# Second attention layer of a two-layer block: queries split where they are made, scores issued one item ahead, the gate product moved to the front, the sums of shares moved to GpSimd

## The chip, the cores and the metric

One Trainium2 chip, one core of it. The metric is device time of one launch in microseconds (us). Engines are named as in the profile: PE is TensorE (PEld its weight loads), DVE is VectorE, ACT is ScalarE, POOL is GpSimd, SP is SyncE, which here issues all the DMAs.

## The reference

A sequence of 1024 rows of 1024 features passes two blocks. The change is in the last attention of the second one, a banded attention with 16 heads of 64, two key/value heads and a sink per head, followed by a gate:

```
def swa_sink_mixer(h, kb, vb, pos_bias, mask, w_in, sinks, w_out):
    q, z = jnp.split(h @ w_in, 2, axis=-1)
    q = q * (HEAD_DIM ** -0.5)
...
    def block_fn(args):
        qn, kn, vn, mn = args
        s = jnp.einsum('bqhgd,bkhd->bhgqk', qn, kn).astype(jnp.float32) + pos_bias
        s = jnp.where(mn[None, None, None], s, NEG_INF)
        m = jnp.maximum(jnp.max(s, axis=-1, keepdims=True), sink)
        p = jnp.exp(s - m)
        p = p / (jnp.sum(p, axis=-1, keepdims=True) + jnp.exp(sink - m))
        return jnp.einsum('bhgqk,bkhd->bqhgd', p.astype(vn.dtype), vn)
...
    return (o * jax.nn.silu(z)) @ w_out
```

Each block of 128 queries sees the 128 keys before it and its own 128, so a row of scores is 256 wide.

## The kernel before

Every product is made in three matmuls: each fp32 operand is held as a high part (`...h`, a copy rounded to fp32r) and a low part (`...l`, the operand minus its high part), and high*high, high*low and low*high are summed in PSUM. ACT makes the high parts, DVE or POOL the low ones.

Every engine has a program written out by hand, stage after stage (`pe_keys`, `act_keys`, ... and then `pe_window`, `act_window`, `dve_window`, `pool_window`, `sp_window`, and then `..._final`). Engines run in order and wait on semaphores by named events: `self.at("q2hi", j)` is the event "high part of query tile j is ready", set where the instruction that makes it says `up(("q2hi", j))`. The SP engine issues DMAs in order and waits in order too.

The projection stage (`..._keys`) makes, after keys and values, 16 units `("b", j)` of 128 features by 1024 rows: units 0 to 7 are queries, units 8 to 15 the gate. ACT copies each from PSUM into one of five tiles `tmp` (queries scaled by 0.125, gate through Silu) and SP stores it in a DRAM scratch `qd`. The weights of each unit are loaded to `raw`, and split into `wh` (ACT) and `wl` (POOL), some units ahead.

The window stage (`..._window`) is a software pipeline over 32 items n = (j, m): query tile j holds two heads, m is a pair of query blocks. `pipeline(32, [(lag, f), ...])` runs step s = 0, 1, ... and in each step calls every f(s - lag) in the order in which the list has them; so in one step an engine works on several items, and the order of the list is the order in its queue. The work on one item, with its lag:

- PE `score` (lag 0): 12 matmuls k2h/k2l by q2h/q2l into two PSUM halves, one for each head.
- DVE `top` (0): four custom instructions (line 103) that add the bias table `t`, negate, write to `tmp` and reduce the row's minimum to `st`.
- POOL `sink` (0): a 128x4 addition. ACT `exps` (0): four Exp with row sums, and one of 128x4 for the sinks.
- DVE `norm` (2): the 128x4 sum of the row sums and the sinks' exponentials, and its reciprocal. POOL `norm` (2): the 128x1024 product of the exponentials with the reciprocal.
- PE `turn` (3): eight transposes into PSUM. ACT `turned` (3): two copies to p2h. DVE `turned_low` (3): two subtractions to p2l.
- PE `values` (4): up to 20 matmuls with the values; two items share one PSUM half.
- Every second item, lag 5: DVE `stored` multiplies the output by the gate tile `zs`, ACT `stored` makes o2h, POOL `stored_low` o2l, SP `zload` reloads `zs` for the next pair, once o2l is made.
- Every fourth item, lag -2 (`begin`): the next query tile, loaded by SP into `tmp[4]`, is split by ACT (q2h) and DVE (q2l). The two pairs of query tiles `qb` alternate. The second pair lies where an operand of the projection was, so it can't be written before unit ("b", 15) is done (`QZ`).

The final stage is the output projection (`("bo", ...)`, matmuls o2h/o2l by wh/wl) and the last normalization.

Of the kernel before, what the change touches and what calls it, by code (L numbers as in the profile page):

```python
# [7 lines left out]
F32 = mybir.dt.float32  # L8
FR = mybir.dt.float32r
ALU = mybir.AluOpType  # L10
# [134 lines left out]
class Net:  # L145
# [36 lines left out]
    def setup(self):  # L182
# [3 lines left out]
        for i in range(6):  # L186
            self.add_slot(3 + i)
        self.tmp = [self.sb(f"tmp{i}", 10 + i) for i in range(5)]
        if "ps" not in self.mem:
            self.mem["ps"] = [self.nc.alloc_psum_tensor(f"ps{i}", [128, S], F32) for i in range(4)]  # L190
        self.halves = [Half(t[:, h * 512:h * 512 + 512]) for t in self.mem["ps"] for h in (0, 1)]
# [94 lines left out]
        self.gates = self.dram("gates", [2048, S])  # L286
        self.xs = self.dram("xs", [S, S])
        self.hd = self.dram("hd", [22 * 128, S])
        self.qd = self.dram("qd", [2048, S])
# [2400 lines left out]
    def sp_keys(self, e):  # L2690
        self.half_units(e, "pl", 256, self.sp_w)
        self.sp_w(e, "k2")
        self.sp_w(e, "v2")
        e.wait_ge(*self.at("kx", 1))
        e.dma_start(self.kx0[64:128, :], self.kx0[0:64, :]).then_inc(self.sig["kx0"].up(("kxt", 0)), 16)
        e.dma_start(self.kx1[0:64, :], self.kx1[64:128, :]).then_inc(self.sig["kx1"].up(("kxt", 1)), 16)
        self.sp_w(e, ("b", 0))
        self.sp_w(e, ("b", 1))
        for j in range(NT):
            for h in (0, 1):  # L2700
                e.wait_ge(*self.at("sum", "n4", h, j))
            e.dma_start(self.xs[j * 128:j * 128 + 128, :], self.X[j][:, :]).then_inc(
                self.sig[f"xs{j}"].up(("xs", j)), 16)
        for j in range(16):
            if j == 3:
                e.wait_ge(*self.at("gst"))
                e.wait_ge(*self.at(*self.POOL_OUT))
                for kv in range(2):
                    self.sp_table(e, f"t2{kv}", self.T2[kv], 8 + 8 * kv)
            if j == 14:  # L2710
                e.wait_ge(*self.at("t3free", 9))
                e.wait_ge(*self.at("qd", 0))
                e.dma_start(self.tmp[4][:, :], self.qd[0:128, :]).then_inc(self.sig["ld4"].up(("ql2", 0)), 16)
            if j >= 2:
                self.sp_w(e, ("b", j))
            i = self.b_tmp(j)
            e.wait_ge(*self.at("bcopy", j))
            e.dma_start(self.qd[j * 128:j * 128 + 128, :], self.tmp[i % 5][:, :]).then_inc(
                self.sig[f"st{i % 5}"].up(("qd", j), ("t3free", i)), 16)

    def b_tmp(self, j):
        return j if j < 14 else j + 1

    def act_keys(self, e):
        for event in self.POOL_TMP:
# [25 lines left out]
        for j in range(16):  # L2751
            if j in (6, 8):
                self.act_flip(e, "t2%d" % (j // 2 - 3), self.T2[j // 2 - 3])
            if j == 10:
                for i in range(NT):
                    e.wait_ge(*self.at("xs", i))
                for kv in (0, 1):
                    self.act_keys2(e, kv)
            if j == 12:
                e.wait_ge(*self.at("zv2"))  # L2760
                e.wait_ge(*self.at("prod", "v2t"))
                for kv in (0, 1):
# [4 lines left out]
            i = self.b_tmp(j)  # L2767
            e.wait_ge(*self.at("prod", ("b", j)))
            if i < 5:
                e.wait_ge(*self.at("nlo", "n4", 3, 1, 6))  # L2770
                e.wait_ge(*self.at("nlo", "n4", 3, 1, 7))
            elif i == 19:
                pass
            else:
                e.wait_ge(*self.at("t3free", i - 5))
            done = self.sig["evac"].up(("bcopy", j), ("free", ("b", j)))
            if j < 8:
                e.activation(self.tmp[i % 5][:, :], self.ps(("b", j)), ACT.Copy, scale=0.125).then_inc(done, 1)
            else:
                e.activation(self.tmp[i % 5][:, :], self.ps(("b", j)), ACT.Silu).then_inc(done, 1)  # L2780

    def act_keys2(self, e, kv):
        e.wait_ge(*self.at("kxt", kv))
# [32 lines left out]
    def dve_keys(self, e):  # L2816
# [10 lines left out]
        for j in range(NT):  # L2827
            e.wait_ge(*self.at("xs", j))
        e.tensor_scalar(self.nsk[:, :], self.sk[:, :], -1.0, None, ALU.mult).then_inc(self.sig["vec"].up(("nsk",)), 1)
        for kv in (0, 1):  # L2830
            self.dve_keys2(e, kv)
        e.wait_ge(*self.at("prod", "v2t"))
# [53 lines left out]
    def pe_window(self, e):  # L2886
# [43 lines left out]
        tiles = sorted(self.pool4, key=lambda i: max(x.taken for x in self.halves[2 * i:2 * i + 2]))  # L2930
        h = [self.halves[2 * i + k] for i in tiles for k in (0, 1)]
        self.p_score, self.p_turn, self.p_out = h[0:4], h[4:7], h[7:8]
        pipeline(32, [(0, score), (3, turn), (4, values)])

    def sp_window(self, e):
        def zload(m):
            e.wait_ge(*(self.at("z2lo", m - 1) if m else self.at("prod", "v2")))
            e.wait_ge(*self.at("qd", 8 + m // 2))
            e.dma_start(self.zs[:, :], self.qd[1024 + m // 2 * 128:1152 + m // 2 * 128, m % 2 * 512:m % 2 * 512 + 512]).then_inc(
                self.sig["zs"].up(("zs", m)), 16)  # L2940

        def stored_low(n):
            if n % 2 and n < 31:
                zload(n // 2 + 1)

        def fetch(n):
            j, m = self.ITEMS2[n]
            if m:
                return
            if j == 0:  # L2950
                zload(0)
            else:
                e.wait_ge(*self.at("q2hi", j - 1))
                e.wait_ge(*self.at("q2lo", j - 1))
                e.wait_ge(*self.at("qd", j))
                e.dma_start(self.tmp[4][:, :], self.qd[j * 128:j * 128 + 128, :]).then_inc(self.sig["ld4"].up(("ql2", j)), 16)

        pipeline(32, [(5, stored_low), (-5, fetch)])

    def act_window(self, e):  # L2960
        def begin(n):
            j, m = self.ITEMS2[n]
            if m:
                return
            e.wait_ge(*self.at("ql2", j))
            if j == 0:
                e.wait_ge(*self.at(*self.POOL_OUT))
            elif j == 1:
                e.wait_ge(*self.at(*self.QZ))
            else:  # L2970
                e.wait_ge(*self.at("prod", ("s2", 4 * j - 5)))
            e.activation(self.qb[j % 2][0][:, :], self.tmp[4][:, :], ACT.Copy).then_inc(self.sig["ahi"].up(("q2hi", j)), 1)

        def exps(n):
            L = self.tmp[n % 4]
            mm, sm, es, rd = self.st2(n)
# [20 lines left out]
                e.activation(self.o2h[j][:, m // 2 * 512:m // 2 * 512 + 512], self.zs[:, :], ACT.Copy).then_inc(  # L2997
                    self.sig["ahi"].up(("z2hi", n // 2)), 1)

        pipeline(32, [(3, turned), (5, stored), (-2, begin), (0, exps)])  # L3000

    def dve_window(self, e):
        vec = self.sig["vec"]

        def begin(n):
            j, m = self.ITEMS2[n]
            if m:
                return
            QH, QL = self.qb[j % 2]
            e.wait_ge(*self.at("q2hi", j))  # L3010
            e.tensor_tensor(QL[:, :], self.tmp[4][:, :], QH[:, :].bitcast(F32), ALU.subtract).then_inc(
                self.sig["vlo"].up(("q2lo", j)), 1)

        def top(n):

# [4 lines left out]
            if n >= 4:  # L3020
                e.wait_ge(*self.at("l2free", n - 4))
            else:
                e.wait_ge(*self.at("t3free", 16))
                e.wait_ge(*self.at("t3free", n + 10 if n != 1 else 11))
            e.wait_ge(*self.at("prod", ("s2", n)))
            for odd, i, k, o in self.each2(n):
                t = (2 * j + odd) % 8 * 256
# [6 lines left out]

        def norm(n):
            mm, sm, es, rd = self.st2(n)
            e.wait_ge(*self.at("exp2", n))
            e.tensor_tensor(sm, sm, es, ALU.add).then_inc(vec.up(("all2", n)), 1)
            e.wait_ge(*self.at("all2", n))
            e.reciprocal(rd, sm).then_inc(vec.up(("share2", n)), 1)  # L3040

# [12 lines left out]
                e.tensor_tensor(self.zs[:, :], self.zs[:, :], self.ps(("o2", n // 2)), ALU.mult).then_inc(  # L3054
                    vec.up(("zmul", n // 2), ("free", ("o2", n // 2))), 1)

        pipeline(32, [(2, norm), (0, top), (5, stored), (3, turned_low), (-2, begin)])

    def pool_window(self, e):
        def norm(n):  # L3060
# [7 lines left out]
        def sink(n):  # L3068
# [3 lines left out]
            e.tensor_tensor(es, mm, self.sk[:, 2 * j:2 * j + 2].unsqueeze(2).to_broadcast([128, 2, 2]), ALU.add).then_inc(  # L3072
                self.sig["gps"].up(("sink2", n)), 1)

        def stored_low(n):
            j, m = self.ITEMS2[n]
            if m % 2:
                hs = slice(m // 2 * 512, m // 2 * 512 + 512)
                e.wait_ge(*self.at("z2hi", n // 2))
                e.tensor_tensor(self.o2l[j][:, hs], self.zs[:, :], self.o2h[j][:, hs].bitcast(F32), ALU.subtract).then_inc(  # L3080
                    self.sig["plo"].up(("z2lo", n // 2)), 1)

        e.wait_ge(*self.at("t3free", 16))
        e.wait_ge(*self.at("t3free", 10))
        for c in (0, 512):
            e.memset(self.tmp[0][:, c:c + 128], 0.0).then_inc(self.sig["gps"].up(("zero2", c)), 1)
        pipeline(32, [(0, sink), (2, norm), (5, stored_low)])

# [266 lines left out]
```

## Time and profile before

| | us |
|---|---|
| median of 3 runs | 2680.98 (2678.99 to 2688.63) |
| the profiled execution: its time, its span | 2687.76, 2686.0 |
| PE busy / DVE / ACT / POOL in the span | 2527.8 / 1705.6 / 967.1 / 650.8 |
| last matmul of the projection ends (the window stage begins) | about 2409.1 |
| first transpose of item 0, of item 28 | 2421.64, 2564.26 |
| first matmul of the output projection | 2580.54 |

Times in the trace count from the span's start. A row of the timeline has the start, the duration, the engine, the line (a helper's: 67 is matmul, 70 transpose, 73 ACT, 76 tensor_tensor, 79 scalar_tensor_tensor, 88 reciprocal, 103 the custom reduction), what is written and read, and in brackets how long the engine sat idle before it and what ended that. Durations of one engine's neighbours overlap a little, since they are pipelined; the distance of two starts is what one costs.

### The profile page before, as it was taken

The page shows a single profiled execution, that of the slowest core. Times are in us where ns is not written, and L with a number is a line of the kernel's source. Part 1 is how long each engine was busy: PE and PEld are TensorE (multiplying, and loading weights), DVE is VectorE, ACT ScalarE, POOL GpSimd, SP SyncE. Part 2 cuts the span into 40 slices and gives each one's busy share as a digit, 9 for nine tenths or more (in the row PEclk, how much of TensorE's full clock was granted, in tenths as well). Part 3 has the DMA queues.
Part 4 walks back from the last instruction along what each step waited for, and adds up shares of the span by engine and source line. Part 5 has one row for each costly group of instructions (what it writes and reads, how often), then busy time and mean ns, then how long its engine had stood idle before and what let it go on. Part 6 is the DMA issues. An engine that isn't in the chain of part 4 may idle for free.

```text
span 2686.0 us, 32097 instructions
## 1 busy us (share of the span) xinstructions
PE 2527.8 (94%) x12224; PEld 2081.1 (77%) x12224; DVE 1705.6 (64%) x2873; ACT 967.1 (36%) x1775; POOL 650.8 (24%) x504
## 2 busy tenths in 40 slices
PE   5899999988999899999999989999999989998898
PEld 3778888777787688888888867888778767777787
DVE  5499999477424887777644378558576572009843
ACT  4431221477223422222311243233243253227732
POOL 2147522476443000000000210000000243315543
PEclk7999999899999899999999999999999989999899
DMA  4112233100454366563623223232273115331143
GB/s 166 48 37 66 79 94 99 51 1 21 168 172 134 94 195 189 173 194 119 228 79 110 79 78 101 96 111 78 95 276 124 61 42 173 94 106 52 41 149 102
DMA packets 260868, 293.72 MB, mean 109 GB/s; under 512 B 10888, under 2 KB 216172, under 8 KB 260716
## 3 DMA queue, kind: packets, MB, share of 16 engines
q1 hardware_dynamic: 260716, 291.66, 33.6%
q8 instruction: 99, 1.62, 0.2%
q14 instruction: 53, 0.43, 0.1%
HBM read 223.95 MB, written 66.10 MB: 108 GB/s over the span
## 4 chain that ended last, share of the span: by engine, by line
PE 79%; DVE 13%; ACT 4%; issue 1%; DMA 1%; POOL 0%; SPq 0%; DVEq 0%; ACTq 0%; POOLq 0%
PE ps L67 78%; PE ps L70 2%; DVE tmp L103 2%; DVE tmp L79 2%; ACT tmp L73 1%; DVE sm L79 1%; DVE tmp L76 1%; ACT pth L73 1%; DVE X L79 1%; DVE pwa L76 1%; DVE wl L76 1%; DVE q2l L76 1%; DVE p2l L76 1%; DVE B2l L76 1%; DVE ptl L79 0%
## 5 line engine op out<-in xcount | busy, mean ns | idle before, releaser
L76 POOL TENSOR_TENSOR wl<-raw,wh 128x512 fp32r<-128x512 f32 (+1 forms) x224 | 291.1, 1321 | 1591.2 <-ACT wh L73 1591.0
L73 ACT ACTIVATE wh<-raw 128x512 fp32r<-128x512 f32 (+1 forms) x388 | 226.4, 621 | 244.1 <-PE ps L67 178.2
L73 ACT ACTIVATE tmp<-ps 128x512 f32<-128x512 f32 (+5 forms) x172 | 127.7, 751 | 391.5 <-PE ps L67 375.3
L67 PE MATMUL ps<-B2h,wh 128*128 128x512 f32 x616 | 245.5, 398 | 12.0 <-DVE B2l L76 6.7
L67 PE MATMUL ps<-B2h,wl 128*128 128x512 f32 x616 | 243.2, 395 | 0.0
L67 PE MATMUL ps<-B2l,wh 128*128 128x512 f32 x616 | 242.9, 394 | 0.0
L76 DVE TENSOR_TENSOR tmp<-tmp,ps 128x512 f32<-128x512 f32 x204 | 138.4, 685 | 109.2 <-PE ps L67 92.8
L67 PE MATMUL ps<-ah,wh 128*128 128x512 f32 (+1 forms) x608 | 192.5, 394 | 14.6 <-DVE xt L85 10.6
L73 ACT ACTIVATE wh<-ws 128x512 fp32r<-128x512 f32 x152 | 94.3, 626 | 291.0 <-DVE ws L76 263.7
L67 PE MATMUL ps<-B3h,wh 128*128 128x512 f32 x448 | 179.8, 401 | 14.8 <-DVE B3l L76 7.4
L67 PE MATMUL ps<-al,wh 128*128 128x512 f32 (+1 forms) x608 | 191.1, 391 | 0.0
L67 PE MATMUL ps<-ah,wl 128*128 128x512 f32 (+1 forms) x608 | 191.0, 391 | 0.0
L67 PE MATMUL ps<-B3l,wh 128*128 128x512 f32 x448 | 177.5, 396 | 0.0
L67 PE MATMUL ps<-B3h,wl 128*128 128x512 f32 x448 | 177.1, 395 | 0.0
L100 DVE MATCH_REPLACE8 sm<-m,sm 128x384 f32<-128x384 f32 (+2 forms) x192 | 166.6, 874 | 0.0
L97 DVE MAX8 m<-sm 128x8 f32<-128x384 f32 (+2 forms) x192 | 160.8, 878 | 0.0
L67 PEld LDWEIGHTS ps<-B2h,wh 128*128 128x128 f32 x616 | 117.3, 190 | 41.6 <-issue 7.7
L67 PEld LDWEIGHTS ps<-ah,wh 128*128 128x128 f32 (+1 forms) x608 | 113.8, 187 | 42.4 <-DVE xt L85 10.8
L76 DVE TENSOR_TENSOR X<-X,ps 128x1024 f32<-128x1024 f32 (+1 forms) x56 | 59.6, 1068 | 131.6 <-PE ps L67 131.5
L67 PEld LDWEIGHTS ps<-B2h,wl 128*128 128x128 f32 x616 | 117.3, 190 | 25.0
L67 PEld LDWEIGHTS ps<-B2l,wh 128*128 128x128 f32 x616 | 117.5, 191 | 24.0 <-issue 0.2
L67 PEld LDWEIGHTS ps<-ah,wl 128*128 128x128 f32 (+1 forms) x608 | 113.9, 187 | 25.0 <-issue 0.9
(290 smaller groups left out, 5848.5 us busy)
## 6 DMA issues: line engine op xcount, KB each, us to landing
ada<-in_ada_w SPq DMA_DIRECT2D x48, 512.0 KB, 3.9
raw<-in_w_in SPq DMA_DIRECT2D x37, 512.0 KB, 4.5
raw<-in_a_w_in SPq DMA_DIRECT2D x33, 512.0 KB, 4.7
gates<-tmp SPq DMA_DIRECT2D x32, 512.0 KB, 3.0
raw<-in_w_ffn_gate SPq DMA_DIRECT2D x24, 512.0 KB, 5.9
hd<-tmp SPq DMA_DIRECT2D x22, 512.0 KB, 4.5
gf<-hd SPq DMA_DIRECT2D x22, 512.0 KB, 7.1
raw<-in_a_w_out SPq DMA_DIRECT2D x20, 512.0 KB, 3.4
```

The lines of the kernel that those rows point to most:

```text
L67: return self.e.matmul(*a, **k) if self.e else Ins()
L70: return self.e.transpose(*a, **k) if self.e else Ins()
L73: return self.e.activation(*a, **k) if self.e else Ins()
L76: return self.e.tensor_tensor(*a, **k) if self.e else Ins()
L79: return self.e.scalar_tensor_tensor(*a, **k) if self.e else Ins()
L97: return self.e.max(*a, **k) if self.e else Ins()
L100: return self.e.match_replace(*a, **k) if self.e else Ins()
L103: return self.e.tensor_tensor_reduce(*a, **k) if self.e else Ins()
```

## The change

1. Queries are split where they are made. For units 0 to 7 ACT writes the scaled high part (tiles `tmpr`, the same memory as `tmp` in type fp32r) and DVE makes the low part from PSUM (`0.125 * ps - high`), both are stored, so `qd` has 3072 rows, and in the window stage SP loads two tiles of 512 KB (`sp_queries`) straight into `qb`. The `begin` steps of ACT and DVE are gone.
2. `score` has lag -1: PE issues the scores of item s+1 ahead of the transposes of item s-3.
3. In DVE's list `stored` (the product with the gate) stands ahead of `top`.
4. The 128x4 sum of `norm` goes from DVE to POOL, at lag 1 (`total`), and POOL's `norm` stands ahead of its `sink`.
5. The first four items wait for fewer stores: `top(n)` for the store of tile 20+n rather than all for that of the last gate unit.

```
-            if j == 14:
-                e.wait_ge(*self.at("t3free", 9))
-                e.wait_ge(*self.at("qd", 0))
-                e.dma_start(self.tmp[4][:, :], self.qd[0:128, :]).then_inc(self.sig["ld4"].up(("ql2", 0)), 16)
+            if j == 10:
+                self.sp_queries(e, 0)
...
+    def b_tiles(self, j):
+
+        if j < 8:
+            return [(2 * j, j, ("bcopy", j)), (2 * j + 1, 16 + j, ("qlow", j))]
+        return [(8 + j, j, ("bcopy", j))]
+
+    def sp_queries(self, e, j):
+
+        for part, (tile, row) in enumerate(zip(self.qb[j % 2], (j, 16 + j))):
+            e.wait_ge(*self.at("qd", row))
+            e.dma_start(tile[:, :].bitcast(F32), self.qd[row * 128:row * 128 + 128, :]).then_inc(
+                self.sig[f"ld{4 + 2 * part + j % 2}"].up((("q2hi", "q2lo")[part], j)), 16)
...
+        for j in range(8):
+            hi, lo = (i for i, _, _ in self.b_tiles(j))
+            e.wait_ge(*self.at("bcopy", j))
+            self.b_tmp_free(e, lo)
+            e.scalar_tensor_tensor(out=self.tmpr[lo % 5][:, :], in0=self.ps(("b", j)), scalar=0.125,
+                                   in1=self.tmpr[hi % 5][:, :].bitcast(F32), op0=ALU.mult, op1=ALU.subtract).then_inc(
+                self.sig["vlo"].up(("qlow", j), ("free", ("b", j))), 1)
...
-        pipeline(32, [(0, score), (3, turn), (4, values)])
+        pipeline(32, [(-1, score), (3, turn), (4, values)])
...
-            else:
-                e.wait_ge(*self.at("q2hi", j - 1))
-                e.wait_ge(*self.at("q2lo", j - 1))
-                e.wait_ge(*self.at("qd", j))
-                e.dma_start(self.tmp[4][:, :], self.qd[j * 128:j * 128 + 128, :]).then_inc(self.sig["ld4"].up(("ql2", j)), 16)
...
+                return
+            if j == 1:
                 e.wait_ge(*self.at(*self.QZ))
             else:
                 e.wait_ge(*self.at("prod", ("s2", 4 * j - 5)))
-            e.activation(self.qb[j % 2][0][:, :], self.tmp[4][:, :], ACT.Copy).then_inc(self.sig["ahi"].up(("q2hi", j)), 1)
+            self.sp_queries(e, j)
...
-        pipeline(32, [(3, turned), (5, stored), (-2, begin), (0, exps)])
+        pipeline(32, [(3, turned), (5, stored), (0, exps)])
...
-            e.wait_ge(*self.at("q2hi", j))
-            e.tensor_tensor(QL[:, :], self.tmp[4][:, :], QH[:, :].bitcast(F32), ALU.subtract).then_inc(
-                self.sig["vlo"].up(("q2lo", j)), 1)
...
-                e.wait_ge(*self.at("t3free", 16))
-                e.wait_ge(*self.at("t3free", n + 10 if n != 1 else 11))
+                e.wait_ge(*self.at("t3free", 20 + n))
...
-            e.wait_ge(*self.at("exp2", n))
-            e.tensor_tensor(sm, sm, es, ALU.add).then_inc(vec.up(("all2", n)), 1)
             e.wait_ge(*self.at("all2", n))
             e.reciprocal(rd, sm).then_inc(vec.up(("share2", n)), 1)
...
-        pipeline(32, [(2, norm), (0, top), (5, stored), (3, turned_low), (-2, begin)])
+        pipeline(32, [(2, norm), (5, stored), (0, top), (3, turned_low)])
...
+        def total(n):
+            mm, sm, es, rd = self.st2(n)
+            e.wait_ge(*self.at("exp2", n))
+            e.tensor_tensor(sm, sm, es, ALU.add).then_inc(self.sig["gps"].up(("all2", n)), 1)
...
-        pipeline(32, [(0, sink), (2, norm), (5, stored_low)])
+        pipeline(32, [(2, norm), (0, sink), (1, total), (5, stored_low)])
```

DVE's queue in the middle of the window stage, before: one step that ends with the split of a query tile, and the next one up to the product with the gate (`tmp_70` to `tmp_73` are the items' tiles).

```order
L76 TENSOR_TENSOR p2l_527<-ps,p2h_526 128x512 x2
L76 TENSOR_TENSOR q2l_529<-tmp_74,q2h_528 128x1024
L76 TENSOR_TENSOR st<-st 128x4
L88 RECIPROCAL st<-st 128x4
L103 ISA tmp_73,st<-ps,t_522,nsk 128x256
...
L76 TENSOR_TENSOR p2l_525<-ps,p2h_524 128x512 x2
L76 TENSOR_TENSOR st<-st 128x4
L88 RECIPROCAL st<-st 128x4
L103 ISA tmp_70,st<-ps,t_523,nsk 128x128
...
L103 ISA tmp_70,st<-ps,t_523,nsk 128x256
...
L76 TENSOR_TENSOR zs<-zs,ps 128x512
```

The same steps of DVE in the changed kernel:

```order
L76 TENSOR_TENSOR p2l_532<-ps,p2h_531 128x512 x2
L88 RECIPROCAL st<-st 128x4
L103 ISA tmp_73,st<-ps,t_527,nsk 128x256
...
L76 TENSOR_TENSOR p2l_530<-ps,p2h_529 128x512 x2
L88 RECIPROCAL st<-st 128x4
L76 TENSOR_TENSOR zs<-zs,ps 128x512
L103 ISA tmp_70,st<-ps,t_528,nsk 128x128
...
L103 ISA tmp_70,st<-ps,t_528,nsk 128x256
```

The split of the query and the 128x4 sum are gone, and the product with the gate has moved from behind the four reductions to ahead of them.

POOL's queue at about the same place, before (three steps):

```order
L76 TENSOR_TENSOR o2l_541<-zs,o2h_533 128x512
L76 TENSOR_TENSOR st<-st,sk 128x4
L76 TENSOR_TENSOR tmp_73<-tmp_73,st 128x1024
L76 TENSOR_TENSOR st<-st,sk 128x4
L76 TENSOR_TENSOR tmp_70<-tmp_70,st 128x1024
L76 TENSOR_TENSOR o2l_542<-zs,o2h_534 128x512
```

And in the changed kernel:

```order
L76 TENSOR_TENSOR o2l_546<-zs,o2h_538 128x512
L76 TENSOR_TENSOR tmp_73<-tmp_73,st 128x1024
L76 TENSOR_TENSOR st<-st,sk 128x4
L76 TENSOR_TENSOR st<-st 128x4
L76 TENSOR_TENSOR tmp_70<-tmp_70,st 128x1024
L76 TENSOR_TENSOR st<-st,sk 128x4
L76 TENSOR_TENSOR st<-st 128x4
L76 TENSOR_TENSOR o2l_547<-zs,o2h_539 128x512
```

In each step the 128x1024 product now stands ahead of the sinks' addition, and the sum (`st<-st`) behind it.

## Rows read from the trace of the kernel before

**Rows 1.** The page: busy time of each engine, and the chain that ended last.
```profile
PE 2527.8 (94%) x12224; PEld 2081.1 (77%) x12224; DVE 1705.6 (64%) x2873; ACT 967.1 (36%) x1775; POOL 650.8 (24%) x504
PE 79%; DVE 13%; ACT 4%; issue 1%; DMA 1%; POOL 0%; SPq 0%; DVEq 0%; ACTq 0%; POOLq 0%
```

**Rows 2.** Stretches: busy us (instructions) by engine, granted clock, DMA share, GB/s.
```profile
2240.00:2409.00 169.00, 168.12 (x724) 136.23 (x723) 3.89 (x6) 39.33 (x54) 49.36 (x37) 0.99 0.36 108
2421.64:2564.26 142.62, 119.32 (x1005) 108.72 (x1005) 122.52 (x358) 102.04 (x330) 73.31 (x69) 0.91 0.15 46
2459.98:2479.09 19.11, 15.69 (x148) 14.26 (x147) 17.58 (x52) 14.69 (x48) 10.65 (x10) 1.00 0.18 57
2479.09:2501.28 22.19, 18.72 (x148) 17.23 (x146) 17.59 (x52) 14.82 (x48) 10.64 (x10) 0.85 0.17 49
```

**Rows 3.** DVE's timeline from 2460.58, four items.
```profile
2460.58 0.15 DVE L76 TENSOR_TENSOR st<-st 128x4 f32<-128x4 f32 x1
...
2463.71 1.02 DVE L76 TENSOR_TENSOR st<-st 128x4 f32<-128x4 f32 x1
...
2468.04 0.43 DVE L76 TENSOR_TENSOR st<-st 128x4 f32<-128x4 f32 x1
2468.50 0.18 DVE L88 RECIPROCAL st<-st 128x4 f32<-128x4 f32 x1
2469.63 0.48 DVE L103 CUSTOM_DVE_ANT_0 tmp<-ps,t,nsk 128x256 f32<-128x256 f32 x1 [0.95 <-PE ps L67]
...
2472.45 1.03 DVE L76 TENSOR_TENSOR st<-st 128x4 f32<-128x4 f32 x1
...
2477.58 2.20 DVE L76 TENSOR_TENSOR q2l<-tmp,q2h 128x1024 fp32r<-128x1024 f32 x1 [0.45 <-ACT q2h L73]
```

**Rows 4.** POOL's timeline at the same place.
```profile
2462.82 1.89 POOL L76 TENSOR_TENSOR tmp<-tmp,st 128x1024 f32<-128x1024 f32 x1
2468.41 1.28 POOL L76 TENSOR_TENSOR o2l<-zs,o2h 128x512 fp32r<-128x512 f32 x1
```

**Rows 5.** Groups of instructions in 2408 to 2580 (busy us, mean ns, idle before).
```profile
L76 DVE TENSOR_TENSOR st<-st 128x4 f32<-128x4 f32 x32 | 21.1, 660 | 0.0
L76 DVE TENSOR_TENSOR q2l<-tmp,q2h 128x1024 fp32r<-128x1024 f32 x8 | 16.9, 2114 | 46.3 <-ACT q2h L73 46.3
L76 DVE TENSOR_TENSOR zs<-zs,ps 128x512 f32<-128x512 f32 x15 | 10.2, 683 | 2.3 <-DMA zs<-qd 1.3 <-PE ps L67 1.0
L73 ACT ACTIVATE o2h<-zs 128x512 fp32r<-128x512 f32 x15 | 9.5, 632 | 6.8 <-DVE zs L76 6.8
L76 POOL TENSOR_TENSOR st<-st,sk 128x4 f32<-128x4 f32 x32 | 6.4, 199 | 77.1 <-DVE st L103 75.7 <-DVE st L76 1.4
```

**Rows 6.** Waits of PE in 2415 to 2575: us in total, times, longest.
```profile
PE ps L67 <- DVE zs L76: 16.8, 13, 1.5
```

**Rows 7.** The start and the end of the window stage, timeline.
```profile
2411.15 1.28 ACT L73 ACT_TABLE_LOAD   x1
2412.54 0.48 PE L67 MATMUL ps<-k2h,q2h 64*128 64x128 f32 x2 [3.41 <-DVE q2l L76]
2417.54 0.18 DVE L88 RECIPROCAL st<-st 128x4 f32<-128x4 f32 x1
2419.69 1.89 POOL L76 TENSOR_TENSOR tmp<-tmp,st 128x1024 f32<-128x1024 f32 x1
2421.64 1.97 PE L70 MATMUL ps<-ident,tmp 128*128 128x128 f32 x8 [2.41 <-POOL tmp L76]
2564.26 1.97 PE L70 MATMUL ps<-ident,tmp 128*128 128x128 f32 x8
2580.54 0.45 PE L67 MATMUL ps<-o2h,wh 128*128 128x512 f32 x1
```

**Rows 8.** DMAs from 2230 on: KB each, median us to landing.
```profile
tmp<-qd SPq DMA_DIRECT2D x8, 512.0 KB, 3.9
zs<-qd SPq DMA_DIRECT2D x16, 256.0 KB, 2.8
```

More of the change, by code:

```diff
@@ L188, in setup @@
         self.tmp = [self.sb(f"tmp{i}", 10 + i) for i in range(5)]
+        self.tmpr = [self.sb(f"tmpr{i}", 10 + i, S, FR) for i in range(5)]
         if "ps" not in self.mem:
@@ L288, in setup @@
         self.hd = self.dram("hd", [22 * 128, S])
-        self.qd = self.dram("qd", [2048, S])
+        self.qd = self.dram("qd", [3072, S])
         self.yd = self.dram("yd", [12 * 128, S])
@@ L2709, in sp_keys, with b_tmp_free @@
                     self.sp_table(e, f"t2{kv}", self.T2[kv], 8 + 8 * kv)
-            if j == 14:
-                e.wait_ge(*self.at("t3free", 9))
-                e.wait_ge(*self.at("qd", 0))
-                e.dma_start(self.tmp[4][:, :], self.qd[0:128, :]).then_inc(self.sig["ld4"].up(("ql2", 0)), 16)
+            if j == 10:
+                self.sp_queries(e, 0)
             if j >= 2:
                 self.sp_w(e, ("b", j))
[L2716 to L2722, printed above, removed]
+            for i, row, event in self.b_tiles(j):
+                e.wait_ge(*self.at(*event))
+                tile = self.tmpr[i % 5][:, :].bitcast(F32) if j < 8 else self.tmp[i % 5][:, :]
+                e.dma_start(self.qd[row * 128:row * 128 + 128, :], tile).then_inc(
+                    self.sig[f"st{i % 5}"].up(("qd", row), ("t3free", i)), 16)
+    def b_tiles(self, j):
[7 more added lines that the diff above has]
+                self.sig[f"ld{4 + 2 * part + j % 2}"].up((("q2hi", "q2lo")[part], j)), 16)
+    def b_tmp_free(self, e, i):
+        if i >= 5:
+            e.wait_ge(*self.at("t3free", i - 5))
+            if i - 5 < 16 and (i - 5) % 2 == 0:
+                e.wait_ge(*self.at("qlow", (i - 5) // 2))
+        else:
+            e.wait_ge(*self.at("nlo", "n4", 3, 1, 6))
+            e.wait_ge(*self.at("nlo", "n4", 3, 1, 7))
     def act_keys(self, e):
@@ L2766, in act_keys @@
                 self.act_w(e, ("b", j))
-            i = self.b_tmp(j)
+            i = self.b_tiles(j)[0][0]
             e.wait_ge(*self.at("prod", ("b", j)))
[L2769 to L2773, printed above, removed]
-            else:
[L2775 to L2778, printed above, removed]
-            else:
-                e.activation(self.tmp[i % 5][:, :], self.ps(("b", j)), ACT.Silu).then_inc(done, 1)
+            self.b_tmp_free(e, i)
+            if j < 8:
+                e.activation(self.tmpr[i % 5][:, :], self.ps(("b", j)), ACT.Copy, scale=0.125).then_inc(
+                    self.sig["ahi"].up(("bcopy", j)), 1)
+            else:
+                e.activation(self.tmp[i % 5][:, :], self.ps(("b", j)), ACT.Silu).then_inc(
+                    self.sig["evac"].up(("bcopy", j), ("free", ("b", j))), 1)
     def act_keys2(self, e, kv):
@@ L2951, in fetch @@
                 zload(0)
-            else:
-                e.wait_ge(*self.at("q2hi", j - 1))
-                e.wait_ge(*self.at("q2lo", j - 1))
-                e.wait_ge(*self.at("qd", j))
-                e.dma_start(self.tmp[4][:, :], self.qd[j * 128:j * 128 + 128, :]).then_inc(self.sig["ld4"].up(("ql2", j)), 16)
[L2958 to L2963, printed above, removed]
                 return
[L2965 to L2968, printed above, removed]
+            if j == 1:
                 e.wait_ge(*self.at(*self.QZ))
@@ L2971, in begin, with act_window @@
                 e.wait_ge(*self.at("prod", ("s2", 4 * j - 5)))
-            e.activation(self.qb[j % 2][0][:, :], self.tmp[4][:, :], ACT.Copy).then_inc(self.sig["ahi"].up(("q2hi", j)), 1)
+            self.sp_queries(e, j)
+        pipeline(32, [(5, stored_low), (-5, fetch)])
+    def act_window(self, e):
         def exps(n):
@@ L2998, in stored @@
                     self.sig["ahi"].up(("z2hi", n // 2)), 1)
-        pipeline(32, [(3, turned), (5, stored), (-2, begin), (0, exps)])
+        pipeline(32, [(3, turned), (5, stored), (0, exps)])
     def dve_window(self, e):
         vec = self.sig["vec"]
[L3005 to L3009, printed above, removed]
-            e.wait_ge(*self.at("q2hi", j))
-            e.tensor_tensor(QL[:, :], self.tmp[4][:, :], QH[:, :].bitcast(F32), ALU.subtract).then_inc(
-                self.sig["vlo"].up(("q2lo", j)), 1)
         def top(n):
@@ L3081, in stored_low @@
                     self.sig["plo"].up(("z2lo", n // 2)), 1)
-        e.wait_ge(*self.at("t3free", 16))
-        e.wait_ge(*self.at("t3free", 10))
+        e.wait_ge(*self.at("t3free", 20))
         for c in (0, 512):
             e.memset(self.tmp[0][:, c:c + 128], 0.0).then_inc(self.sig["gps"].up(("zero2", c)), 1)
-        pipeline(32, [(0, sink), (2, norm), (5, stored_low)])
+        pipeline(32, [(2, norm), (0, sink), (1, total), (5, stored_low)])
     WINDOWED = (("pv2", 31), ("z2lo", 15), ("z2hi", 15), ("soft2", 31), ("p2lo", 31, 1))
```

## The prediction

> **What bounds the kernel now.** I read the page first: PE is busy for 94% of the span and takes 79% of the chain that ended last [rows 1]. The matmuls are not touched by the change, so it can only give what PE waits for, or runs through at its lower clock, in the stage that changes. The stretches show where that is. In the projection, 2240 to 2409, PE is busy for 168.12 of 169.00 us at a granted clock of 0.99, and DVE for 3.89 us [rows 2]. In the window stage, from the first transpose of item 0 (2421.64) to that of item 28 (2564.26), 28 items take 142.62 us, 5.09 each; PE is busy for 119.32 of them and the clock is 0.91, which is a mixture of 2.4 and 1.2 GHz [rows 2]. The four items from 2459.98 ran wholly at 2.4 GHz: 19.11 us, of which DVE was busy for 17.58, PE for 15.69 and ACT for 14.69; the next four took 22.19 with the same DVE work and a clock of 0.85 [rows 2]. DVE's own idle time in the first four is one wait of 0.95 for PE and one of 0.45 for ACT [rows 3], so DVE paces this stage, PE is next, and the low clock comes on top.
>
> Why DVE is that busy is seen in its timeline. The 128x4 sum takes 0.15 us at one place and 1.02, 0.43 and 1.03 at the others [rows 3]. POOL's product runs from 2462.82 for 1.89 us, to 2464.71, and the sum that starts at 2463.71 ends at 2464.73: it ends when POOL does [rows 3, 4]. Over 32 items the sums take 21.1 us, the eight query splits 16.9 [rows 5]. A reciprocal that starts at 2468.50 takes its 0.18 beside POOL's 1.28 us subtraction from 2468.41 [rows 3, 4], so it isn't held.
>
> The Trainium skill (SBUF — State Buffer, section "Who interferes with whom") says that a VectorE tensor_tensor with both inputs in SBUF and a GpSimd operation exclude each other, and the later one waits for the whole of the other. The trace agrees for the sums (1.02 against 0.15). Without that reading only 32 times 0.15, 4.8 us, would be DVE's gain from the moved sums.
>
> **The change part by part.**
>
> *Sums to POOL.* In the four items the sums take 0.15 + 1.02 + 0.43 + 1.03 = 2.63 us of DVE [rows 3]; all of it goes. POOL gets 32 additions like its own for the sinks, 0.20 each [rows 5]; it is busy for 10.65 of 19.11, so 0.8 more is hidden. The sum now stands behind the next item's sink addition, which waits for that item's reductions, and o2l and the next product are queued behind it. As the reciprocal is only asked for a step later, this has nearly a step of slack.
>
> *Query split.* 2.20 us of DVE and its 0.45 wait go from each four items [rows 3]; ACT loses the copy. In their place come eight 128x1024 operations of DVE in the projection, where it is busy for 3.89 of 169 us [rows 2]; each should be no dearer than the split was (2.11, held by POOL included [rows 5]) and no cheaper than two of the 128x512 products with a PSUM input (2 x 0.68 [rows 5]): 11 to 17 us in all, beside PE. Without that cover they would cost this much. The eight further stores of 512 KB there go on SP's queue ahead of the next weight load, which they hold back by one such operation a unit, under 2.2 us of the 11 us or so of a unit (169 us hold between 15 and 16 of the 16 units); weights are fetched units ahead, so nothing. In the window stage SP issues 14 loads instead of 7 for tiles 1 to 7. They are asked for five items ahead; landing was 3.9 for one of 512 KB [rows 8], at most 7.8 for two one behind the other, against 5 items of 3.9: hidden, except for tile 1, which can't be loaded before the projection ends.
>
> *Scores ahead.* The 0.95 wait of DVE goes, as the scores of an item are there a step early. What is left of DVE's four items is 19.11 - 2.63 - 2.20 - 0.45 - 0.95 = 12.9 us, 3.2 an item. PE needs 15.69, 3.92 an item. PE becomes the bound.
>
> *Gate first.* PE waits 16.8 us, 13 times, for the product with the gate, which frees the PSUM half [rows 6]; before, it stands behind four reductions that wait for PE's scores. Now it stands at the front and PE has scores and transposes to do meanwhile. What is queued behind it on DVE, the reductions, now waits for the values of the pair and for `zs`; with 0.7 us an item to spare that is absorbed.
>
> *Steady part.* 28 items at 3.92 are 109.8 us. Handovers that remain: between nothing and what PE waited before at the front of a transpose or a value (some 0.2 an item); I take 0.1, 3 us. Low clock: in the four items after 2479.09 it cost 22.19 - 19.11 = 3.1 us, and over the 28 items about 142.62 - 7 x 19.11 = 8.9. It set in where PE sat idle before, and in the projection, busy throughout, it doesn't; with PE busy almost throughout I take a third, 3 us, bounds 0 and 9. So 115.8 instead of 142.6: -26.8.
>
> *Start.* PE waited 3.41 us for the first split [rows 7]; this goes. Then the reciprocal of item 0 was issued at 2417.54, but POOL started the product at 2419.69, as the sink addition of item 2 stood ahead [rows 7]; now the product is ahead, about 2 us. Against it stand the scores of item 4 ahead of the first transposes, which need tile 1, loaded behind the projection's end (2 x 3.9 bounds it at about 2418). ACT's table load (1.28 [rows 7]) starts 1 us earlier, as its query copy is gone. I take -4.5, bounds -2 and -6.
>
> *End.* From the transposes of item 28 to the output projection 16.28 us [rows 7], no scores in it; less low clock, -1, bounds 0 and -2.
>
> Sum: -26.8 - 4.5 - 1 = -32.3 us. The profiled execution was 2687.76, 6.8 above the median; against its own time that makes 2655.5, against the median 2648.7. The output projection is PE's own, so what is gained ahead of it stays. I forecast 2648.
>
> **The rivals.**
>
> *PE takes over, as above:* 2638 to 2655, chance 0.58.
>
> *The round of zs or the handovers pace it, about 4.4 us an item.* A pair of items now turns round this ring: product with the gate 0.68, o2h 0.63, o2l 1.28, reload 2.8 [rows 4, 5, 8], together 5.4, but o2h stands behind two copies that wait for PE's transposes, and o2l behind POOL's sum and sink, which wait for the reductions; these put about 2 us more in. That is 7.4 against 7.84 for two items of PE. If the reload lands in 3.9 instead of 2.8, as the 512 KB loads do that are now doubled, the pair takes 8.5, 4.25 an item, and the reductions queued behind the product are late with it. At 4.4 an item: 123.2 + 3 = 126.2, -16.4, with start and end -21.9: 2659. For it speaks how near the ring is, against it that the reload was waited for by only 1.3 us so far [rows 5]. Chance 0.23.
>
> *The clock takes it.* If PE at the bound gets 0.85 all the way, as in the stretch from 2479.09, an item takes 3.92 / 0.85 = 4.61, 28 take 129, -13.6; with a start and end of -3: 2664. At a mean 0.8 it would be 137, -5.4, and 2672. For it: the clock went down in this stage although PE was busy for 84% of it; against: it stays at 0.99 under full load. The Trainium skill (TensorE: Matmul & The Clock Gate, section "A second HAM failure mode: psum-queue depth-cycling") tells of a kernel whose short idle pieces between groups of matmuls let the clock swing between its two levels; by that rule the small waits left here would be enough, and this rival's time would hold. Chance 0.11.
>
> *The stage stays as it is:* PE's 5.09 is not DVE's doing, and only start and split move: about -5, 2676. Against it stands DVE's 17.58 of 19.11. Chance 0.04.
>
> *Slower.* The product with the gate, now first, makes DVE wait for `zs` in every pair. To lose the 5.5 us of start and end too, 28 items must take over 148, 10.6 a pair, so the reload must land in 10.6 - 4.6 = 6.0 us instead of 2.8, behind two query loads in the same queue. At 6.5, 11.1 a pair makes 155: +13 - 5.5, 2688. Only 7 of 14 pairs have query loads near. Chance 0.04, to which no case gives more.
>
> **How the numbers follow.** A measurement of this kernel can tell about 0.5%, 13 us, from no change: faster means below 2667.6. The first two cases are (0.81), three quarters of the clock's (0.08), and a little of the rest (0.02): 0.91. Same: the rest of the clock's, the stage that stays, part of the last: 0.06. Slower 0.03. The range runs from 2636 (109.8 with nothing lost, the start at -6, the end at -2, is -41, 2640, and some scatter) to 2667, into the clock's case: it leaves out 0.15. The likeliest case's own is 2638 to 2655.
>
> **What the changed profile would show.** No 128x4 sum on DVE; POOL's takes 0.2 and none of DVE's instructions of one size is longer than its like. Four items at clock 1.00 in 15.7 to 16.3 us with PE busy for 15.7, DVE for about 13. No wait of 3.4 ahead of the first scores, first transposes some 8 us behind the projection's end instead of 12.5. PE's wait for zs gone. The projection as before, with PE busy throughout. I would be wrong if DVE waits for `zs` by its DMA in each pair, if the granted clock of the stage falls to 0.85, if the projection shows PE waiting, or if the first scores of a tile wait for q2h or q2l.

## The result

The changed kernel takes 2642.79 us (median of 4 runs, 2639.89 to 2647.45) against 2682.41 of the kernel before beside it: the ratio is 0.9851, 95% interval 0.9826 to 0.9877, so 39.6 us less. The forecast was 2648.

The profiled execution's span is 2638.1 us, 47.9 below that of before. Of this, 5.3 us lie ahead of the window stage, where only the added operations of the projection differ: the projection ended at 2409.1 and now ends at 2403.8. I don't count them to the change, as the kernel with early scores alone, which has the old projection, ends it at 2404.8, nearly as early (its first scores start at 2408.17 after a wait of 3.41). The median shows 39.6 in all.

The stretches of the changed kernel (columns as in [rows 2]): the projection, the start of the window stage, the 28 items, and four of them.

```profile
2235.00:2403.00 168.00, 167.12 (x721) 135.68 (x721) 13.69 (x14) 39.34 (x54) 49.55 (x39) 0.99 0.42 136
2403.80:2414.10 10.30, 4.97 (x61) 4.18 (x60) 6.71 (x34) 8.39 (x29) 5.00 (x9) 0.95 0.78 277
2414.12:2517.48 103.36, 103.36 (x995) 97.56 (x993) 88.25 (x314) 90.85 (x315) 75.39 (x94) 0.99 0.24 83
2443.29:2458.32 15.03, 15.03 (x148) 14.21 (x146) 12.88 (x47) 13.26 (x47) 11.38 (x15) 1.00 0.32 106
```

The projection is as full as before, with DVE at 13.69 us instead of 3.89. The 28 items take 103.36 us instead of 142.62, PE is busy in all of it, at 0.99 instead of 0.91. Four items take 15.03 instead of 19.11 [rows 2]; DVE's 12.88 in them is the 12.9 that was worked out.

The waits of the changed kernel from 2405 to 2545 (us, times, longest), those of PE and DVE that matter:

```profile
DVE zs L76 <- DMA zs<-qd: 9.8, 10, 4.7
...
PE ps L67 <- DMA q2l<-qd: 3.6, 1, 3.6
...
PE ps L67 <- DVE zs L76: 0.9, 2, 0.5
...
PE ps L70 <- POOL tmp L76: 0.3, 1, 0.3
```

PE's 16.8 us of waiting for the gate [rows 6] are 0.9. DVE does wait for `zs` by its load, but PE doesn't feel it. The start and the end, timeline:

```profile
2403.86 0.33 PE L67 MATMUL ps<-k2h,q2h 64*128 64x128 f32 x2
...
2408.83 1.89 POOL L76 TENSOR_TENSOR tmp<-tmp,st 128x1024 f32<-128x1024 f32 x1 [0.29 <-DVE st L88]
...
2412.82 0.33 PE L67 MATMUL ps<-k2h,q2h 64*128 64x128 f32 x2 [3.63 <-DMA q2l<-qd]
...
2414.12 1.97 PE L70 MATMUL ps<-ident,tmp 128*128 128x128 f32 x8
...
2532.40 0.45 PE L67 MATMUL ps<-o2h,wh 128*128 128x512 f32 x1
```

The first scores come at once (3.41 us of waiting before, [rows 7]). The product of item 0 ends at 2410.72, but its transposes start 3.4 us later: the scores of item 4 now stand ahead of them, tile 1 lands only at 2412.8, and these scores take 1.3 us more. The landing times (KB, median us) explain it: two loads of 512 KB at once take longer than the 3.9 of one [rows 8].

```profile
q2h<-qd SPq DMA_DIRECT2D x8, 512.0 KB, 4.5
q2l<-qd SPq DMA_DIRECT2D x8, 512.0 KB, 5.4
zs<-qd SPq DMA_DIRECT2D x16, 256.0 KB, 2.8
```

### The profile page after: what moved, and what is told of

Read it like the earlier page. It is cut to its first block, busy times and chain, and to the rows that moved or that the text cites. A ratio compares the mean times of both kernels' runs of the same rounds, so it can differ in the third digit from the quotient of the medians.

```text
span 2638.1 us, 32127 instructions
## 1 busy us (share of the span) xinstructions
PE 2502.7 (95%) x12224; PEld 2062.3 (78%) x12224; DVE 1677.6 (64%) x2841; ACT 955.5 (36%) x1767; POOL 655.4 (25%) x536
## 4 chain that ended last, share of the span: by engine, by line
PE 80%; DVE 10%; ACT 4%; DMA 2%; issue 2%; POOL 1%; SPq 0%; POOLq 0%; DVEq 0%; ACTq 0%
PE ps L67 78%; PE ps L70 2%; DVE tmp L79 2%; ACT tmp L73 1%; DVE sm L79 1%; DVE tmp L76 1%; ACT pth L73 1%; DVE wl L76 1%; DVE pwa L76 1%; DVE B2l L76 1%; DVE X L79 0%; DVE ptl L79 0%; ACT bh L73 0%; DVE bl L79 0%; ACT wh L73 0%
## 5 line engine op out<-in xcount | busy, mean ns | idle before, releaser
L73 ACT ACTIVATE tmp<-ps 128x512 f32<-128x512 f32 (+5 forms) x164 | 119.2, 738 | 332.3 <-PE ps L67 317.7
L67 PEld LDWEIGHTS ps<-B2h,wl 128*128 128x128 f32 x616 | 116.6, 189 | 24.8
L67 PEld LDWEIGHTS ps<-ah,wl 128*128 128x128 f32 (+1 forms) x608 | 113.7, 187 | 24.8 <-issue 0.6
```

The lines of the kernel that those rows point to most:

```text
L67: return self.e.matmul(*a, **k) if self.e else Ins()
L73: return self.e.activation(*a, **k) if self.e else Ins()
```

## The experiments

In the first four kernels one part is added to the kernel before, in the next four one part is taken back from the changed one. "Start" is from the first scores to the first transposes, "28 items" from the transposes of item 0 to those of item 28, both from each kernel's timeline of PE. The ratio is to runs of the kernel before beside each kernel (medians 2682.41, 2683.92, 2684.12 and 2684.20), and differences below come from it where two kernels weren't run together. With early scores the 28 items hold the scores of one item less (about 1 us), which fall into the start.

| kernel | median us | ratio to before | start | 28 items |
|---|---|---|---|---|
| before | 2680.98 to 2684.2 | | 9.1, after a wait of 3.4 | 142.6 |
| changed | 2642.79 | 0.9851 (0.9826 to 0.9877) | 10.3 | 103.4 |
| changed, again | 2640.62 | 0.9836 (0.9816 to 0.9855) | 10.4 | 103.1 |
| before + early scores | 2681.00 | 0.9988 (0.9977 to 0.9999) | 11.1, after 3.4 | 138.3 |
| before + sums on POOL | 2673.37 | 0.9956 (0.9941 to 0.9971) | 7.6, after 3.4 | 134.2 |
| before + split queries | 2667.85 | 0.9938 (0.9921 to 0.9955) | 8.6 | 128.7 |
| before + gate first | 2676.17 | 0.9975 (0.9963 to 0.9988) | 9.1, after 3.4 | 135.9 |
| changed - early scores | 2641.01 | 0.9836 (0.9821 to 0.9851) | 6.9 | 105.7 |
| changed - sums on POOL | 2657.87 | 0.9899 (0.9884 to 0.9914) | 10.3 | 119.4 |
| changed - split queries | 2663.50 | 0.9916 (0.9900 to 0.9933) | 9.9, after 3.4 | 120.6 |
| changed - gate first | 2642.90 | 0.9844 (0.9829 to 0.9859) | 9.9 | 105.9 |
| changed, one-input sums on DVE, POOL's old order | 2655.27 | 0.9896 (0.9871 to 0.9922) | 10.4 | 118.1 |
| changed - early scores - gate first | 2671.10 | 0.9951 (0.9934 to 0.9968) | 6.9 | 135.0 |
| changed + tile 1 earlier | 2638.73 | 0.9828 (0.9809 to 0.9848) | 7.5 | 102.9 |

### Early scores, alone and taken back

```
-        pipeline(32, [(0, score), (3, turn), (4, values)])
+        pipeline(32, [(-1, score), (3, turn), (4, values)])
```

> The kernel before, with only the scores issued one item ahead. Theory A (DVE's work paces the stage, held by POOL in part; PE takes over only when DVE is relieved): only DVE's waits for PE go, 0.95 us in four items; 28 items fall from 142.6 to about 130 to 137, total 5 to 12 us less, and DVE stays busy for over 90% of the stage. Rival B (the order of the queues is the cause: DVE and PE take turns, and the early scores alone undo it): 28 items in 104 to 112 us, total 30 us or more less.

> The changed kernel, with the scores back at lag 0. Theory A (PE is the bound of the changed kernel, and DVE has 0.5 us an item to spare): DVE waits for each item's scores, but nothing PE does is late; total within 4 us of the changed kernel. Rival B (the early scores carry the gain): 20 us or more slower than the changed kernel.

Alone they give 0.12%, less than either theory had. In the trace the transposes of three items follow each other in 3.3 to 5.2 us, and then one takes 7.5, six times over. Waits of PE there, 2410 to 2570:

```profile
PE ps L67 <- DVE q2l L76: 10.0, 6, 1.7
PE ps L67 <- DVE zs L76: 9.3, 7, 1.3
```

A new wait took part of the gain: early scores need the split query an item sooner, and the split stands at the end of DVE's step. The wait for the gate is cut to 9.3 us from 16.8, and 10.0 for the split are new. Taken back from the changed kernel they cost nothing that the intervals tell (0.9836 against 0.9836 and 0.9851): 2.3 us more in the 28 items (1 of them the scores of item 4), 3.4 less at the start, as item 4's scores are then not ahead of the first transposes.

### Gate first, alone and taken back

```
-        pipeline(32, [(2, norm), (0, top), (5, stored), (3, turned_low), (-2, begin)])
+        pipeline(32, [(2, norm), (5, stored), (0, top), (3, turned_low), (-2, begin)])
```

> The kernel before, with only the product with the gate ahead of the reductions. Theory A: PE's 16.8 us of waiting for it go, but DVE has as much to do as before and paces: total 0 to 5 us less. Rival B (PE's waits are what counts): about 17 us less.

> The changed kernel, with the product with the gate back behind the reductions. Theory A: DVE has time to spare, PE has scores and transposes to do meanwhile, and the reductions don't wait for zs; total within 4 us of the changed kernel. Rival B (the early product carries PE's gain): 10 to 17 us slower.

Alone 7.8 us by the medians (3 to 10 by the interval, which reaches into the 0 to 5 of theory A), half of the rival's 17; taken back nothing. An edit that takes no work from DVE gives something to a stage that DVE was said to pace. It doesn't refute DVE as a bound: DVE is busy for 131.3 of the 135.9 us there, as its sums are held for longer (32.2 us in all instead of 21.1 [rows 5]). PE no longer waits for the gate, but for POOL's products (2415 to 2565):

```profile
PE ps L70 <- POOL tmp L76: 23.8, 18, 2.4
```

### Split queries, alone and taken back

The edit is the first part of the diff, with the waits for the stores.

> The kernel before, with only the queries split in the projection and loaded as two parts (with the fewer waits for stores in the first four items). Theory A: DVE loses 2.65 us in four items and the start 3.4 us; total 8 to 20 us less, the projection itself as long as before. Rival B (order): only the start, 3 to 5 us less. If the eight new operations or the stores cost PE anything, the projection shows PE below 168 of 169 us.

> The changed kernel, with the queries loaded whole and split in the window stage by ACT and DVE as before. Theory A: 2.2 us of DVE in each four items and the wait at the start come back: 28 items in 112 to 120 us instead of 103.4, the start 3.4 us longer, total 12 to 20 us slower than the changed kernel. Rival B: the start alone, 3 to 6 us slower.

Alone 16.1 us, and 17 to 22 us lost when taken back: the largest part, at the top of theory A's 12 to 20 or slightly beyond it. The changed kernel's projection, with all of the added operations, has PE busy for 167.12 of 168.00 us: they cost nothing.

### Sums on POOL, alone and taken back

```
-            e.wait_ge(*self.at("exp2", n))
-            e.tensor_tensor(sm, sm, es, ALU.add).then_inc(vec.up(("all2", n)), 1)
...
-        pipeline(32, [(0, sink), (2, norm), (5, stored_low)])
+        pipeline(32, [(2, norm), (0, sink), (1, total), (5, stored_low)])
```

> The kernel before, with only the 128x4 sums moved to POOL (and POOL's product ahead of its sink addition). Theory A: DVE loses 2.6 us in four items of 19.1, part of which comes back as waiting for PE's scores; total 6 to 16 us less. Rival B (order): DVE's wait for the scores grows by what the sums gave up, total 0 to 4 us less.

> The changed kernel, with the 128x4 sums back on DVE. Theory A (they are held by POOL's product): they take 0.6 to 1 us each again instead of 0.15, DVE paces at 4.2 to 4.5 us an item, total 10 to 18 us slower than the changed kernel. Rival B: 32 additions of 0.15, within 4 us.

Alone 10.5 us, and 13 to 17 us lost when taken back; both times are as theory A expected, though not for its reason, as the next kernel shows. Groups in the kernel with the sums back, 2403 to 2560:

```profile
L76 DVE TENSOR_TENSOR st<-st 128x4 f32<-128x4 f32 x32 | 29.6, 926 | 0.3 <-ACT st L73 0.2
```

But the edit has two halves, the place of the sum and the order of POOL's queue. The next kernel has the sum on DVE in a form that POOL shouldn't hold, and POOL's old order.

### One-input sums on DVE

```
-            e.tensor_tensor(sm, sm, es, ALU.add).then_inc(vec.up(("all2", n)), 1)
+            c = (n % 4) * 32
+            e.tensor_reduce(rd, self.st[:, c + 4:c + 12].rearrange("p (t k) -> p k t", t=2), AXX, ALU.add).then_inc(
+                vec.up(("all2", n)), 1)
             e.wait_ge(*self.at("all2", n))
-            e.reciprocal(rd, sm).then_inc(vec.up(("share2", n)), 1)
+            e.reciprocal(rd, rd).then_inc(vec.up(("share2", n)), 1)
```

> The changed kernel with the sums on DVE, as in the kernel with the sums back, but made by a reduction with one input (the row sums and the sinks' exponentials read as one strided view) in place of an addition of two. Theory A (what holds DVE is two inputs in SBUF beside POOL's work): the 32 sums take 0.1 to 0.25 us each and the total is within 4 us of the changed kernel. Rival C (any small DVE operation in this place waits for POOL, or for ACT's last exponential, whatever its inputs): they take 0.5 us or more and the total is 10 to 18 us slower than the changed kernel, as with the sums back.

Each theory is right on one half. The sums take 0.15 us each, as theory A said (its group, 2403 to 2560):

```profile
L106 DVE TENSOR_REDUCE st<-st 128x4 f32<-128x8 f32 x32 | 4.8, 152 | 0.3 <-ACT st L73 0.2
```

One beside POOL's product, in its timeline, with the reciprocal that this product needs:

```profile
2457.66 0.18 DVE L88 RECIPROCAL st<-st 128x4 f32<-128x4 f32 x1
...
2461.24 0.20 POOL L76 TENSOR_TENSOR st<-st,sk 128x4 f32<-128x4 f32 x1 [3.18 <-DVE st L103]
...
2461.39 1.89 POOL L76 TENSOR_TENSOR tmp<-tmp,st 128x1024 f32<-128x1024 f32 x1
...
2462.28 0.15 DVE L106 TENSOR_REDUCE st<-st 128x4 f32<-128x8 f32 x1
...
2462.46 0.18 DVE L88 RECIPROCAL st<-st 128x4 f32<-128x4 f32 x1
...
2463.34 1.09 PE L70 MATMUL ps<-ident,tmp 128*128 128x128 f32 x8 [0.55 <-POOL tmp L76]
```

So what holds DVE is an addition of two SBUF tensors beside POOL's; with one input in place of two it isn't held. (The edit changes the operation too, from an addition of two tensors to a reduction, so the two aren't told apart by it.) The Trainium skill (SBUF — State Buffer, section "Who interferes with whom") has tensor_reduce as never contending on this chip; the trace agrees, 0.152 us on average over 32.

Yet the ratio is 0.9896, against 0.9899 with the held sums: 24.8 us of DVE's busy time came free and bought nothing that the intervals tell (0.8 us by the ratios, 1.3 in the 28 items, 2.6 by the medians). The rows show why. The product at 2461.39 needs the reciprocal that was done at 2457.84. It stands behind the sink addition, which waits for the reductions of an item two further on, with POOL idle for 3.18 us, so it starts 3.55 us late, and the transposes wait for it. Counted over the stage, 30 of the 32 products start 1.6 to 4.6 us behind their reciprocal here, and 1.6 to 3.3 with the held sums; in the changed kernel, which has the product ahead, each of the 32 starts within 1 us. PE waits for such products (2405 to 2550, the kernel with one-input sums):

```profile
PEld ps L70 <- POOL tmp L76: 13.0, 14, 1.6
...
PE ps L70 <- POOL tmp L76: 10.2, 13, 1.4
```

In the changed kernel, with the product ahead, the wait of the same line is 0.3. The sum's place itself costs DVE 0.3 us of waiting. What is left to explain the 13 to 15 us is POOL's order. That follows by elimination and from these rows; the kernel with the sums on DVE and POOL's new order wasn't run, so what the held sums would cost with that order is open.

### Both orders taken back

> The changed kernel without two of its parts: scores at lag 0 and the product with the gate behind the reductions; left are the split queries and the sums on POOL. Theory A (relief of DVE is all that counts, and each of the two orders alone came back without loss): within 5 us of the changed kernel, 28 items in 104 to 110 us. Rival D (the two orders stand in for each other, one of them is needed): 8 us or more slower, PE waiting for the product with the gate in each pair.

```
-        pipeline(32, [(-1, score), (3, turn), (4, values)])
+        pipeline(32, [(0, score), (3, turn), (4, values)])
...
-        pipeline(32, [(2, norm), (5, stored), (0, top), (3, turned_low)])
+        pipeline(32, [(2, norm), (0, top), (5, stored), (3, turned_low)])
```

Each of the two was worth nothing in the changed kernel; without both it loses 1.0 to 1.2%, 27 to 31 us, as rival D expected. Its stretch of 28 items, and PE's wait for the gate in it (2412 to 2547):

```profile
2412.31:2547.27 134.96, 115.77 (x1005) 106.27 (x1005) 90.18 (x322) 96.57 (x329) 81.06 (x100) 0.92 0.22 76
```

```profile
PE ps L67 <- DVE zs L76: 18.1, 13, 1.9
```

DVE is busy for 67% only, relieved as in the changed kernel, and the stage is slow all the same, so DVE's work isn't what paces it. Timeline of one item:

```profile
2462.73 0.39 PE L67 MATMUL ps<-k2h,q2h 64*128 64x256 f32 x2
...
2463.64 1.09 PE L70 MATMUL ps<-ident,tmp 128*128 128x128 f32 x8
...
2463.85 0.48 DVE L103 CUSTOM_DVE_ANT_0 tmp<-ps,t,nsk 128x256 f32<-128x256 f32 x1 [0.94 <-PE ps L67]
...
2465.48 0.68 DVE L76 TENSOR_TENSOR zs<-zs,ps 128x512 f32<-128x512 f32 x1
...
2466.21 0.39 PE L67 MATMUL ps<-p2h,v2c 128*128 128x256 f32 x1 [1.49 <-DVE zs L76]
...
2468.41 0.39 PE L67 MATMUL ps<-k2h,q2h 64*128 64x256 f32 x2
...
2469.32 1.09 PE L70 MATMUL ps<-ident,tmp 128*128 128x128 f32 x8
```

It is a ring over two queues: scores (0.9), reductions (1.84 with the handover), product with the gate (0.73), values (2.2), and the next scores stand behind the values. From transposes to transposes it takes 5.68 us, where PE has 3.9 us of work; in one pair of two the reductions are shorter and it takes 4.74. Early scores cut it in one place (the reductions no longer wait for them), gate first in another (the values no longer wait for the reductions), and one cut is enough.

How little DVE's work counts while the ring stands is seen in the rounds of four items that ran at a granted clock of 1.00 (columns as in [rows 2]): with the split queries alone, with the sums on POOL alone, and with both, as here.

```profile
2430.11:2448.54 18.43, 15.70 (x149) 14.26 (x147) 15.71 (x50) 13.63 (x46) 10.66 (x10) 1.00 0.24 87
2455.07:2473.32 18.25, 15.54 (x148) 14.25 (x146) 14.35 (x48) 14.57 (x48) 11.49 (x14) 1.00 0.19 58
2509.31:2527.57 18.26, 15.55 (x148) 14.26 (x146) 12.90 (x46) 13.63 (x46) 11.45 (x15) 1.00 0.26 88
```

DVE's busy time goes from 17.58 [rows 2] to 15.71, 14.35 and 12.90, and the round only from 19.11 to 18.43, 18.25 and 18.26. The changed kernel, with the same 12.9 of DVE and the ring cut, takes 15.03.

### Tile 1 earlier

```
+            if j == 15:
+                e.wait_ge(*self.at("bused", self.first[self.unit_no[("b", 15)]]))
+                self.sp_queries(e, 1)
```

> The changed kernel, with the second pair of query tiles where the projection's operand is read in the first half of a unit (and the transposed shares in its old place), so that tile 1 is loaded half a unit before the projection ends. PE waits 3.6 us for that load ahead of the first transposes, whose input was there 3.4 us earlier. If that wait is what holds the start: total 3 to 4 us less than the changed kernel. If the start has a chain of its own behind it: 0 to 1 us less.

> The changed kernel once more, for comparison on the same chip: 0.985 of the kernel before.

The start falls from 10.4 to 7.5 us; the load is no longer waited for, and what is left ahead of item 4's scores is a wait for the reductions.

```profile
2411.54 0.33 PE L67 MATMUL ps<-k2h,q2h 64*128 64x128 f32 x2 [1.32 <-DVE st L103]
```

The medians differ by 1.9 us, less than the 3 to 4 expected if the wait alone held the start and more than the 0 to 1 of the other case. The runs of the two (2637.70 to 2639.72, 2640.05 to 2641.64) don't meet, but the intervals of their ratios to before overlap, so 2 to 3 us is what the trace shows and the runs suggest. It is the fastest of the kernels here.

## Why the prediction was right, point by point

**The total.** 39.6 us less against 32.3 forecast in the sum; the time lies in the likeliest case's range. In part that is luck: what held the stage was read only half right (below), but the term that the sum used, PE's own time with little to wait for, is where the stage ends whatever held it before. PE took over as the bound; neither did the clock fall nor the reload of `zs` pace the stage.

**Steady part: right, too small.** -26.8 was forecast, -39.3 measured. Three terms were too high. 3.92 us an item came from PE's busy time in a stretch with waits; without waits four items take 15.03, and the 28 take 103.4 instead of 109.8 (7 x 15.03 is 105.2; about 1 us more went because item 4's scores moved into the start, and the first item has no values to make). Handovers were 3 and are about nothing. Low clock was 3 and is about nothing (0.99).

**What bounds the kernel: the step that failed.** "So DVE paces this stage, PE is next" was read from DVE's 17.58 busy of 19.11 us. It is at most half of it. From transposes to transposes the four items of [rows 3] took 4.79, 4.63, 4.11 and 5.58 us in the kernel before. The second and the fourth, those with a wait for the gate, are the ring with and without the shorter reductions; the kernel with both orders taken back has these same items at 4.7 to 4.8 and 5.7 with DVE far from full. The first and the third end in transposes that start 0.06 us behind POOL's product, which itself starts 1.9 and 2.9 us behind its reciprocal; with POOL's new order they take 3.9. DVE's extra work lay largely within these waits. The forecast held because the change relieves DVE and POOL and cuts the ring as well. For the kernel without the two orders the same sum would have given 32 us less than before, as it has no term for them but DVE's 0.95; measured were 13, so it would have been some 19 us too low. The opposite kernel, both orders without any relief, wasn't run; that each relief taken back still costs 13 to 22 us with the orders in place says that it would keep part of the loss.

**Sums to POOL.** Their being held is shown, and with POOL's old order it is worth 1 to 3 us, which the intervals can't tell from nothing, not what 2.63 us in each four items would say. POOL's order, which the prediction counted only at the start (2 us), is by elimination worth 13 to 15 us, more than the rest of that edit.

**Query split: right.** Hidden in the projection, 16 us alone. Its exception, tile 1, was named: it was bounded at 8.9 us behind the projection's end and came at 9.0.

**Scores ahead, gate first.** "The 0.95 wait of DVE goes" was a small part of what the early scores do, and the 16.8 us of PE's waiting were counted nowhere by themselves; the two are one effect, worth some 30 us together where DVE and POOL are relieved, nothing when one of them is taken back, and 2.9 and 7.8 us when added alone.

**Start and end.** -4.5 forecast, -2.2 measured (12.5 to 10.3): the product came sooner as said, and the load of tile 1 took most of it back. The bound for that load was right; that 1.3 us of scores follow it ahead of the first transposes was left out. End -1, measured -1.4 (14.9 instead of 16.3).

**Rivals.** Of the ring of `zs` it is right that DVE now waits for the load, 9.8 us in 10 waits; the prediction called such a wait in each pair a sign of being wrong, but it is within DVE's spare time and PE waits 0.9 us for the gate in all. Of the clock: it rose from 0.91 to 0.99 with PE busy throughout. The Trainium skill (TensorE: Matmul & The Clock Gate, section "A second HAM failure mode: psum-queue depth-cycling") tells of a swing between two levels where short idle pieces stand between groups of matmuls; the trace agrees for the kernel before (1.00 and 0.85 in [rows 2]), and the small waits left in the changed one brought no such swing. Waits alone don't set it: with one-input sums PE was idle for 12.3 of 118.1 us and the clock was 0.99 too. Eight transposes take 1.09 us in the record at a granted clock of 1.00, and 1.97 at 0.50.

**Open.** Whether POOL's order alone gives all of the 13 to 15 us. And why the granted clock differs between kernels with as many waits: split queries alone have 0.97 and both orders taken back 0.92. The second, with more relief, takes 135.0 us for its 28 items against 128.7; their rounds at 1.00 are alike (18.26 and 18.43), so the difference lies in the rounds at a lower clock.

## What to carry to other kernels

When an engine is busy for 92% of a stretch, don't yet call it the bound: write down the ring of queue orders (who stands behind whom on each engine) and add up its durations; here 4.7 or 5.7 us of ring stood in every second item beside DVE's work, and a late product of POOL in the others. Of two edits that cut the same ring each showed nothing when taken back alone, so take back pairs as well. In an in-order queue put what only needs old data ahead of what waits for new data: on POOL this order was, by elimination, worth far more than the held additions that the profile showed. To find such a place, compare when an operation starts with when its input was done.

## What was not expected of the hardware

A two-input 128x4 addition on DVE beside POOL's operation took 1.02 us in many places and 1.25 at most instead of 0.15, while a one-input reduction over the same eight numbers took 0.15 beside it, and the reciprocal 0.18. (The 1.25 is from the kernel with only the gate first.) PE's busy time overstates its work where it stops often: 15.69 us for four items before, 15.03 for the same matmuls when they run without a stop, both at full clock. Two 512 KB loads issued together landed in 4.5 and 5.4 us (medians) where one took 3.9.
